# Two more groups of U transposed by DMA, four up tiles behind the gate stage, and high halves of products later in the loop

## The reference, cut to what matters

```python
def peer(xn, wq, subkeys, u, v):                      # 512 tokens, D = 1024
        q = (xb @ wq).reshape(t, PEER_HEADS, 2, PEER_DQ // 2)
        s = jnp.einsum('thpd,hpkd->thpk', q, subkeys)   # 128 keys a half
        s_top, i_top = lax.top_k(s, K)                  # K = 16
        cand = (s_top[:, :, 0, :, None] + s_top[:, :, 1, None, :]).reshape(t, PEER_HEADS, K * K)
        c_top, c_idx = lax.top_k(cand, K)
        i1 = jnp.take_along_axis(i_top[:, :, 0], c_idx // K, axis=-1)
        i2 = jnp.take_along_axis(i_top[:, :, 1], c_idx % K, axis=-1)
        e = i1 * N_KEYS + i2
        g = jax.nn.softmax(c_top, axis=-1)
        act = jax.nn.gelu(jnp.einsum('thkd,td->thk', u[e], xb), approximate=False)
        return jnp.einsum('thk,thkd->td', g * act, v[e])
```

## Time and profile before

| | us |
|---|---|
| median of 3 runs | 2203.56 |
| lowest, highest | 2201.19, 2205.31 |
| the profiled execution, whole | 2197.33 |
| its span in the trace | 2195.5 |
| up tiles 0 to 31 on PE | 1008 to 1133 |
| gate stage | 1136 to 1283 |
| loop | from about 1327 |

### The profile page before, as it was taken

How to read it: one execution, slowest core, us unless ns; L and a number is a source line. 1 busy time by engine, 2 the same in 40 slices (tenths; PEclk the granted TensorE clock), 3 DMA queues, 4 the chain that set the end, 5 groups by cost and what they waited for, 6 DMA issues and landing times.

```text
span 2195.5 us, 29225 instructions
## 1 busy us (share of the span) xinstructions
PE 2077.8 (95%) x11066; PEld 1147.8 (52%) x11218; DVE 1502.7 (68%) x2689; ACT 827.5 (38%) x1225; POOL 1081.2 (49%) x610
## 2 busy tenths in 40 slices
PE   8999899999989999889999988989999999999998
PEld 4446544444444456445666754545544555555554
DVE  2668555545541654695998968778887788888764
ACT  3232343323331444311137754333333434444442
POOL 1001346566545334861302227666666667677761
PEclk9999999999999999999999999999999999999999
DMA  7020438989974114996949999888887888888852
GB/s 236 0 105 12 154 117 242 258 245 248 254 224 150 66 53 137 252 295 170 329 155 390 379 339 344 307 309 309 311 306 286 306 304 302 307 308 285 317 185 83
DMA packets 277575, 514.90 MB, mean 235 GB/s; under 512 B 131122, under 2 KB 188726, under 8 KB 266436
## 3 DMA queue, kind: packets, MB, share of 16 engines
q1 hardware_dynamic: 232516, 367.90, 50.5%
q0 software_dynamic: 36864, 134.23, 17.8%
q10 hardware_dynamic: 8064, 11.01, 1.5%
HBM read 416.09 MB, written 67.65 MB: 220 GB/s over the span
## 4 chain that ended last, share of the span: by engine, by line
PE 25%; DVE 13%; DMA 11%; POOL 7%; issue 4%; ACT 1%; ACTq 0%; DVEq 0%; POOLq 0%; SPq 0%
PE ps L2166 8%; DMA arena<-in_peer_u,small 6%; PE ps L2091 6%; PE ps L2118 5%; DMA arena<-in_peer_v,small 4%; PE ps L2154 3%; POOL split L948 3%; POOL arena L937 3%; DVE arena L2829 2%; DVE x_sb L2833 2%; DVE arena L2938 2%; PE ps L2108 1%; DVE arena L2964 1%; DVE arena L2811 1%; PE ps L1787 1%
## 5 line engine op out<-in xcount | busy, mean ns | idle before, releaser
L2166 PE MATMUL ps<-split,arena 128*128 128x512 bf16 x1606 | 371.8, 384 | 4.8 <-DVE arena L2979 1.5
L948 POOL TENSOR_TENSOR split<-ring,split 128x1024 bf16<-128x1024 f32 x128 | 297.1, 2324 | 64.6 <-ACT split L1364 62.8
L2118 PE MATMUL ps<-arena 128*128 128x384 bf16 x1728 | 297.8, 330 | 10.6 <-ACT u_split L1371 9.9
L821 POOL TENSOR_TENSOR split<-ring,split 128x4096 bf16<-128x4096 f32 x26 | 207.2, 7969 | 193.3 <-ACT split L1146 191.0
L1787 PE MATMUL ps<-arena,split 128*128 128x512 bf16 x1316 | 296.5, 380 | 5.9 <-DVE arena L2610 2.0
L937 POOL DMA_INDIRECT arena<-in_peer_u,small x128 | 159.8, 1249 | 257.5 <-DVE arena L2829 240.2
L2166 PEld LDWEIGHTS ps<-split,arena 128*128 128x128 bf16 x1656 | 163.8, 99 | 186.4 <-issue 10.5
L2833 DVE SCALAR_TENSOR_TENSOR x_sb<-arena,small,x_sb 128x1024 f32<-128x1024 f32 x128 | 205.2, 1603 | 71.7 <-DMA arena<-in_peer_v,small 69.9
L2118 PEld LDWEIGHTS ps<-arena 128*128 128x128 bf16 x1728 | 170.4, 99 | 122.4 <-issue 17.5
L2829 DVE SCALAR_TENSOR_TENSOR arena<-arena,bcast 128x1024 f32<-128x1024 f32 x128 | 176.5, 1387 | 80.1 <-DMA arena<-in_peer_u,small 79.5
L1787 PE MATMUL ps<-split,arena 128*128 128x512 bf16 x1034 | 229.6, 381 | 1.2
(11 more groups left out here) (341 smaller groups left out, 3145.7 us busy)
## 6 DMA issues: line engine op xcount, KB each, us to landing
ring<-in_peer_v SPq DMA_DIRECT2D x32, 2048.0 KB, 12.8
ring<-in_peer_u SPq DMA_DIRECT2D x18, 2048.0 KB, 17.1
ring<-in_w_ff SPq DMA_DIRECT2D x16, 2048.0 KB, 8.6
arena<-in_peer_u SPq DMA_DIRECT2D x56, 512.0 KB, 4.8
turned_table<-u_split SPq DMA_DIRECT2D x56, 512.0 KB, 5.6
ring<-turned_table SPq DMA_DIRECT2D x14, 2048.0 KB, 10.4
gate_matrix<-split SPq DMA_DIRECT2D x12, 2048.0 KB
arena<-gate_matrix SPq DMA_DIRECT2D x32, 768.0 KB
```

The source lines that it names most:

```text
L821: pool.tensor_tensor(split[:, s4 % 2, 1, :], ring[:, (s4 + 5) % RING, :], split[:, s4 % 2, 0, :], ALU.subtract).then_inc(w_lo, 1)
L948: pool.tensor_tensor(split[:, s % 2, 1, at], ring[:, s % 2, at], split[:, s % 2, 0, at], ALU.subtract).then_inc(v_lo, 1)
L2118: mm = pe.matmul(up_bank, a, b, start=n == 0, stop=n == len(terms) - 1)
L2166: mm = pe.matmul(down_bank(t, c), a, w, start=s == 0 and j == 0 and n == 0, stop=s == EX_GROUPS - 1 and j == 3 and n == 2)
```

## The change

- `PRE` is 16: groups 14 and 15 are turned in advance too, 64 chunks in place of 56. Their eight fills each on PE, with ACT's copies and DVE's lows, are gone (`FILLS = 128`, before 144). All fills now use the raw copies of ACT. The new pairs 28 to 31 stand on SP between the loads of turned groups 7 to 10, and on POOL after the sums.
- `SELECTED` is 28: the picks are awaited at tile 27. The gate stage has 24 tiles as before (28 to 51), and tiles 52 to 55 stand behind it.
- SP's loads of U for the live groups come later in the list: group 16 waits for the tiles of group 14, group 17 for those of group 15.
- In the loop `live_high(g, 2)` and `(g, 3)` move into the next step, `live_high(g, 0)`, `(g, 1)` and the stored ones stand later on ACT, and DVE's order follows.
- `pair_up` writes its casts side by side; `pair_keys` runs over as many elements in the order that this gives. `places` holds 256 values instead of 32.

```diff
-        SELECTED, GATED, EARLY = 32, 24, 14
+        SELECTED, GATED, EARLY = 28, 24, 14
         LIVE = EX_GROUPS - EARLY
-        PRE = EARLY
+        PRE = 16
...
-        top_pairs = part(arena, 2048, NT, 2, TOPK, 2 * P_HEADS, dt=BF16)
-        place_pairs = part(arena, 13568, TOPK, 2, dt=BF16)
+        top_pairs = part(arena, 2048, NT, 2 * P_HEADS, TOPK, 2, dt=BF16)
+        places = part(arena, 13568, TOPK, TOPK, dt=BF16)
...
         def fill_place(f):
-            return EARLY + f // 8, f // 2 % 4, f % 2
-        FIRST = 8
+            return PRE + f // 8, f // 2 % 4, f % 2
+        FILLS = 8 * (EX_GROUPS - PRE)
...  SP
-            for p in range(24, 2 * PRE):
-                pre_pair(p, p < 2 * PRE - 1)
+            for p in range(24, 28):
+                pre_pair(p, True)
                 slot_free(p - 24)
                 load_turned(p - 20)
-            for g in (8, 9, 10):
+            pre_pair(28, True)
+            for p, g in ((29, 8), (30, 9), (31, 10)):
+                pre_pair(p, p < 2 * PRE - 1)
                 slot_free(g - RING)
                 load_turned(g)
             for n in range(TD // TB):
...
                 if n == 5:
                     slot_free(10)
-                    load_u(EARLY)
+                    load_turned(EARLY)
                 if n == 8:
                     slot_free(11)
-                    load_u(EARLY + 1)
+                    load_turned(EARLY + 1)
...
             for i in range(EARLY):
                 s = 2 * i
-                sp.wait_ge(u_turned, 8 * i + 8)
-                load_u(EARLY + i + 2)
+                if i == 0:
+                    slot_free(EARLY)
+                    load_u(PRE)
+                if i >= 2:
+                    sp.wait_ge(u_turned, 8 * (i - 2) + 8)
+                    load_u(EARLY + i + 2)
                 sp.wait_ge(stored_mul, 4 * i + 4)
                 load_gates(s + 2)
...
+                if i == 1:
+                    slot_free(EARLY + 1)
+                    load_u(PRE + 1)
...  POOL
             sums(2)
+            pre_late(28)
             sums(3)
+            for p in range(29, 2 * PRE):
+                pre_late(p)
...  ACT, step i of the loop
                 v_high(s, 2)
+                if i > 1:
+                    live_high(g - 1, 2)
                 live_gelu(g, 0)
                 u_high(f)
                 v_high(s, 3)
+                if i > 1:
+                    live_high(g - 1, 3)
                 u_high(f + 1)
-                stored_high(i, 0)
                 v_high(s + 1, 0)
                 live_gelu(g, 1)
+                stored_high(i, 0)
+                u_high(f + 2)
                 stored_high(i, 1)
-                live_high(g, 0)
-                u_high(f + 2)
-                stored_high(i, 2)
                 v_high(s + 1, 1)
                 live_gelu(g, 2)
                 u_high(f + 3)
+                stored_high(i, 2)
+                live_high(g, 0)
+                u_high(f + 4)
                 stored_high(i, 3)
-                live_high(g, 1)
-                u_high(f + 4)
                 v_high(s + 1, 2)
                 live_gelu(g, 3)
-                live_high(g, 2)
+                live_high(g, 1)
                 u_high(f + 5)
                 v_high(s + 1, 3)
                 u_high(f + 6)
-                live_high(g, 3)
...  PE
             for m in range(SELECTED + GATED, 4 * EARLY):
-                turn_fill(m - THREE)
                 early_tile(m)
...  DVE
-                own.did(dve.tensor_copy(top_pairs[:, :, n % 2, :, n // 2 * 2:n // 2 * 2 + 2],
+                own.did(dve.tensor_copy(top_pairs[:, :, n % 2 * P_HEADS + n // 2, :, :],
                                         top_i[:, :, n, :].unsqueeze(3).to_broadcast([P, NT, TOPK, 2])))
```

188 lines of the change are left out of this document (82 added, 106 removed).

## The result

The changed kernel takes 2255.1 us (median; 2249.7 to 2259.9), beside 2202.4 us (2199.8 to 2205.3) for the kernel before on the same chip: a ratio of 1.024, 95% interval 1.0225 to 1.0263, so 53 us more. Forecast were 2222.6 us, within 2196 to 2243. The sign was right, the size was not: 33 us of the loss were not in the sum. The profiled execution took 2253.4 us, with a span of 2251.5 (before 2195.5).

A forecast was written before the change was run, and what follows sets the result against it. PE was taken to bound most stretches (2077.8 of 2195.5 us busy), DVE with its gathers the loop to 1680. Terms -4 + 22 + 10 + 1 + 0 - 2 - 8 = +19 on 2203.6 gave 2222.6 us, range 2196 to 2243.

The forecast's parts named there:

- Part 1: Gate stage: eight fills of PE's turns of groups 14 and 15 go, -4 us (-5 to 0).
- Part 2: Ahead of the gate stage: SP's four added pairs of DMA transposes land late, delaying its start, +22 us (+5 to +32).
- Part 3: 28 up tiles ahead: PE waits for the picks, ready by 1137 at the latest, before the transposes land; adds nothing.
- Part 4: Gate stage: SP's slot wait delays storing block 6, +10 us (7 to 17); blocks 1, 3, 5, 9 +1 (0 to 5).
- Part 5: Compact casts ahead of the picks: long casts wait for POOL, not spacing, 0 (7.5 us gained to 1 lost).
- Part 6: Gate stage's end to the loop: lighter DVE queue -4, later U loads +2, sum -2 us (-6 to +6).
- Part 7: Loop: later high halves end PE's stalls and shrink POOL's wait for ACT, -8 us (-25 to +10).
- A: Loop: late high halves cut a ring of ACT, POOL and DVE waits, -45 instead of -8, 2186 us; chance 0.15.
- B: Ahead of the gate stage: transposes keep up at 14 to 15 us a pair, picks bound, 2210 us; chance 0.12.
- C: Late loads of U (16 and 17) hold PE's turns in steps 1 and 2, splits push picks, +20, 2243; chance 0.08.
- three signs of being wrong: DVE passes the transposes without stopping; no ACT gate-block wait over 5 us; PE idles under 15 us up to row 128.

The follow-up runs named there:

- the loads moved: Changed kernel with the gate stage's five table loads on SP behind blocks 1, 3, 5, 7, 9 instead of 0, 2, 4, 5, 8: 2223.4 us.
- half rows: Only half of each gathered row of U from the 17th on, output not the reference's: changed kernel 2227.3 us, kernel before 2182.6 us.
- the three repairs: Changed kernel with gate-stage table loads behind blocks 1, 3, 5, 7, 9, SP's pairs ahead, and old loop order in steps 1 to 6: 2199.7 us.

## Why the prediction was right or wrong

**Part 1, fills gone: right.** -4 forecast; with the loads moved the gate stage takes 137.3 us, 6.2 less than before, and 5.2 less with 32 tiles ahead.

**Part 2, the transposes: right in mechanism and near in size.** Forecast: last transposes from 1138.5, landed at 1151, gate stage at 1158.2, +22. Timelines of SP and DVE after, which answer and the earlier trace rows:

```profile
1021.47 8.43 SPq L610 DMA_TRANSPOSE u_split<-u_split  x2
...
1041.95 7.62 SPq L610 DMA_TRANSPOSE u_split<-u_split  x2
...
1133.98 10.70 SPq L610 DMA_TRANSPOSE u_split<-u_split  x4
```

```profile
1140.46 0.69 DVE L2913 TENSOR_TENSOR arena<-arena,small 128x512 f32<-128x512 f32 x1
1146.68 0.29 DVE L2918 CAST u_split<-consts 128x256 bf16<-128x256 f32 x1 [5.26 <-DMA u_split<-u_split]
```

The pace was as read off, 20.5 us for pair 25, and DVE took 7.15 us from its copy to PE's first gate step, where 7.2 were forecast. Of the 4.5 us too many, 2.5 are in the start (pair 25 began at 1021.5, not 1024.0), and 3.1 in pair 30, which took 16.9 us and not 20; pair 29, with 15.4 and not 14, gave 1.4 of it back: +17.7 in place of +22.

**Part 3, the picks: the bound was broken.** "1137 at the latest" was 1141.2. The comparisons and additions L2872, L2879 and L2884 took 45.9 us in place of 35.4 beside POOL's added splits (10.5, forecast 7 to 10). They take 35.4 with the casts alone, so it isn't their new order. The bound counted only these: DVE's other instructions between the sums and the end of the picks took 5 us more as well, up to 2.4 us in place of 0.6 for one. Against it, DVE got POOL's first sums 2.2 us sooner (1044.7 for 1046.9). The late picks cost nothing here, since the transposes came 5 us later still. But DVE's wait for these sums stood in the trace of before, in its waits of 1000 to 1141:

```profile
DVE arena L2795 <- POOL arena L920: 29.1, 1, 29.1
```

Had I read it, I would have seen that the picks, too, hang on SP's wait for its first slot.

**Part 4, the block on SP: the step that failed.** I forecast one late store, block 6, at +10, and gave blocks 1, 3, 5 and 9 +1 together, because their load had "two tiles, 12 us, until needed". Measured are +22.5 us in the stage, +26.5 with the -4 of part 1 taken out. Block 6 by itself was right: ACT waited 15.6 us for it (forecast 14), PE 12.5 (forecast 10). The step that failed is the +1 for the others: ACT waited 4.0, 7.0, 4.0 and 6.0 us for blocks 1, 3, 5 and 9, and PE 8.6 us in all. The order of stores and loads was right; wrong was the time in hand. The five stores took 15.5 to 18.5 us from issue to landing, so a margin of 12 us isn't one. I had 13.5 us for the landing in the same paragraph and didn't put it against the 12. The other missing term is the clock, which the sum had at nothing: the longer stalls were followed by stretches at half clock, worth 7 us of PE's work.

**Part 5, the casts: right.** 0, shown by the run with the casts alone, and by its long cast that ends with POOL's split. By the rule of the Trainium skill (SBUF — State Buffer, Who interferes with whom) cited in the prediction this is what was to be expected; this run agrees, 7.19 us beside 0.23.

**Part 6, from the gate stage to the loop: -2 forecast, +3.9 measured** up to the first down tile, and 3.7 more up to row 30. I had counted the gates' way through memory (27 us) against 31 us of PE's work and let the lighter DVE win 4. But PE's four tiles, in order ahead of the first down tile, bound: 34.0 us from the last gate step to the first down tile, 30.7 with 32 tiles ahead. The 3.7 us to row 30 stay open: from the first down tile to row 30 it was 22.9 us before and 26.5 in the changed kernel, again 22.8 with the loads moved and 22.9 with half rows, but 26.1 with the three repairs.

**Part 7, the high halves: the sign was wrong for the half that I argued with.** -8 forecast, +10.2 from row 30 to 128 and -1.9 from there on. "DVE with its gathers sets the pace" held, and so did the gain at POOL (12.2 us of waiting for ACT gone) and the unchanged sum of DVE's work (272.8 and 277.9 us). What I took from it was wrong: DVE's own order decides when a row buffer comes free, and the change moved DVE's rows together to help POOL. The bound named in passing, "DVE's tail of seven rows in a row is now denser", is where the time went, as far as POOL's waits tell. Order alone is 7 of the 10 us by the runs on the changed kernel; the other 3 (349.7 with the old order, 346.8 before) are less than two runs of the same loop differ by (346.8 and 352.1).

**The rivals.** A (the loop breaks loose) did not come: PE's wait for ACT went, and the row buffers kept the step. B did not: the transposes did not keep up. C named a worse case but with other causes (U of groups 16 and 17 late); PE waited 1.2 us for U in the loop. And of the three signs of being wrong none came: DVE stopped 5.3 us for the transposes, ACT waited 15.6 us for a block, and PE idled 51 us in the loop up to row 128. All three watched for a smaller loss than forecast, none for a larger one.

**The range** broke because each of the parts 4, 6 and 7 was given its bound but not all at once: their upper ends, 17 + 5, 6 and 10, with parts 1 to 3 as they measured, give 52, about what came.

## What to carry to other kernels

When a stage's tiles are moved, move the list of the DMA queue with them: a wait for a slot that is over when it is reached costs nothing, and with the tiles four later the same loads cost 32 us, since each then left just ahead of a store that others wait for. For every store in an in-order queue compare the time until it is needed with its measured landing behind a load, not with the work in between. When executions of the same code differ by 5 us in a piece, a cause of 3 to 7 us wants more than one trace. Before work is put under a wait, ask whether the wait belongs to a ring of buffers; if it does, the work delays the ring's next turn.

## What the runs showed of the hardware

- The last four transposes on SP's queue took it 6.4 us to issue with no table load ahead of them; with one ahead, 10.7 us in the changed kernel, and 18.3 and 23.1 us in two others. In these two ACT stored activations at the same time, but it did so in the first as well. To DVE's release it was 14.8 us without a table ahead and 12.7 us in the changed kernel, so the issue time alone doesn't tell when they land.
- A store of a gate block (2 MB) issued 0.36 us behind a table load of 2 MB on SP's queue landed 15.5 to 18.5 us later, in five cases of the changed kernel. With the load 11 us ahead of the next store, ACT waited 0.7 and 1.5 us.
- A gate stage in which PE stood for ACT at five places was granted a mean clock of 0.92; without these stalls the same work had 0.99. The clock was at half for 6.8, 13.6 and 3.4 us at the stalls of 3.9, 12.5 and 2.9 us, and full in between.
- Halving the gathered rows (2 KB a partition in place of 4) took 20 us off 98 rows, 0.2 us a row, in either order: a round of four buffers falls from 14.2 to 13.3 us (before), so most of a round isn't what the size of the transfer adds, as far as half a row can tell.
